# Gate and up biases of 32 experts issued as four products on two row groups, and the scatter's products in alternate order

## The chip, the cores and the metric

The kernel runs on one core of a Trainium2 chip. Its time is the time on the device, in microseconds (us), from the start of the program to its end; lower is better. All times of the trace are of one execution taken by the hardware profiler.

## The reference, cut to what matters

The program is a chain of two transformer blocks on 256 tokens of width 1024: attention and a mixture of experts, then a second block with gated mixers and key-value lookups. Only the mixture of experts is touched. A router picks 4 of 32 experts for each token, with a softmax over the four scores as weights; each expert is a gated feed-forward layer with biases:

```python
def expert_block(args):
    xb, e = args
    gt = xb @ w_gate[e] + b_gate[e]
    up = xb @ w_up[e] + b_up[e]
    gt = jnp.minimum(gt, SWIGLU_LIMIT)
    up = jnp.clip(up, -SWIGLU_LIMIT, SWIGLU_LIMIT)
    hdn = gt * jax.nn.sigmoid(SWIGLU_ALPHA * gt) * (up + 1.0)
    return hdn @ w_down[e] + b_down[e]
...
contrib = ys[dest] * gates.reshape(-1)[order][:, None].astype(ys.dtype)
out = jax.ops.segment_sum(contrib, tok, num_segments=n_tok)
```

All weights are 1024 x 1024 in float32, and all products are float32.

## The kernel before

**Stages.** `program` (line 2998) runs six stages one after the other: `attention`, `route`, `moe`, `peer`, `gla`, `peer`. Each is a block of its own, with one instruction list per engine: TensorE (`pe`), VectorE (`dve`), ScalarE (`act`), GpSimd (`pool`) and SyncE (`sp`), which issues the large DMAs. An engine takes its list in order and waits on semaphores (`wait_ge`). At the end of a block all engines meet.

**Weights.** They stream through a ring of 2 MB slots in SBUF (class `Ring`, line 128): six slots, and five from expert 26 on. SyncE issues the load of a chunk (line 145) as soon as the slot has been given back by the product that read it last. An expert has six chunks: 0 and 1 for gate, 2 and 3 for up, 4 and 5 for down. Eight experts (3, 5, 8, 11, 15, 17, 23, 25) have one more, for work on the context tokens that `Context` (line 745) puts beside the experts.

**An expert on TensorE** (`expert`, in `moe`, from line 1315). 64 slots hold the tokens that chose it. `x.xe` holds their rows, turned. Every product with weights uses 64 columns of the array: the left half of the output's 1024 columns goes to partitions 0 to 63 of a PSUM bank, the right half to partitions 64 to 127 of the same bank, so each weight row gives two products of 512 columns (`halves`, line 1290, products at L1296). In order:

- gate: the biases into bank 4 (L1327), then chunks 0 and 1. The bias product has `x.select` as its stationary operand, [32 rows, 64 columns], of which row e is ones and the others zeros, and the bias table of all 32 experts as its moving operand, [32 rows, 512 columns]; so it writes expert e's bias into all 64 slots. It starts the accumulation in the bank.
- up: the same into bank 5, with chunks 2 and 3. Ahead of its biases stand the wait for `h_ready` of the expert before (VectorE has read bank 5) and `context.wait_left(pe, 5)`, which waits until the work beside the experts has given back bank 5.
- `gather` (L1278) of the next expert's tokens into bank 7, with the one-hot `x.pick`.
- four transposes of `x.h` (L1340) into bank 6.
- `scatter` (L1287) of the expert before: outputs `x.ye`, left halves on rows 0 to 63 and right halves on rows 64 to 127, are added to four accumulators in banks 0 to 3 with `x.weighT` as the stationary operand, [64 rows, 128 columns]. Two products have rows 0 to 63 (token tiles 0 and 1), two have rows 64 to 127.
- two products that turn the weights of this expert's slots (L1347) into bank 4.
- work beside the expert, if there is some (L176, L818, L847, L890), into banks 5 and 7.
- down: chunks 4 and 5 into bank 6.

**On the other engines.** VectorE clamps bank 4 (L1458), makes the one-hots for scatter (L1440), multiplies with the sigmoid (L1463), clamps bank 5 (L1465), makes `x.h` (L1468), copies the next `x.select` out of the identity matrix (`select`, L1435) and makes the next `x.pick` (L1430). ScalarE does the sigmoid (L1391) and copies banks 7, 6, 4 and 6 to SBUF (L1385, L1394, L1398, L1405); the context's results are emptied by ScalarE (L899) or VectorE (L1019, L1033).

**Tables.** `Experts` (line 1051) lays out the arena. `b_gate` and `b_up` are two areas of 1024 columns, each on partitions 0 to 31, loaded in `route` by two DMAs of SyncE's queue. `constants` (line 223) builds a table of constants that is loaded once; its last part, `zero`, is 128 columns wide and is read nowhere.

A second to fourth pass over the experts (`overflow`) runs only when an expert has more than 64 tokens. It does not run in the profiled execution.

The lines of the biases:

```python
for c in range(4):
    bank = 4 + c // 2
    if c % 2 == 0:
        pe.wait_ge(M(name(("weighT_ready", "h_ready")[c // 2], p)), at(p, e, 1))
        if c == 2:
            context.wait_left(pe, 5)
        for n in range(2):
            nc.tensor.matmul(m.ps[n * SLOTS:(n + 1) * SLOTS, bank, :],
                             x.select[0:NE, :],
                             (x.b_gate, x.b_up)[c // 2][0:NE, n * 512:(n + 1) * 512],
                             start=True, stop=False, skip_group_check=True)
```

Of the kernel before, what the change touches and what calls it, by code (L numbers as in the profile page):

```python
# [21 lines left out]
P = 128  # L22
D = 1024
KT = D // P
T = 256
TT = T // P
# [12 lines left out]
NE, TOPK, SLOTS = 32, 4, 64  # L39
# [15 lines left out]
class Marks:  # L55


    def __init__(self, nc, ctx):
        self.nc, self.ctx, self.sems, self.n, self.spare = nc, ctx, {}, {}, []
# [163 lines left out]
def constants():  # L223

    j, i = np.arange(P)[:, None], np.arange(P)[None, :]
    same = (j // CH) == (i // CH)
    parts = {
        "ident": (j == i),
        "upto": (j <= i),
        "ones": np.ones((P, P)),  # L230
        "fwd": (j <= i) & same,
        "bwd": (j >= i) & same,
        "after": (j > i) & same,
        "before": (j < i) & same,
        "chunk": j // CH == np.arange(2)[None, :],
        "iota": np.broadcast_to(np.arange(P) % CH, (P, P)),
        "zero": np.zeros((P, P)),
    }
    return parts

# [810 lines left out]
class Experts:  # L1051


    def __init__(self, m):
        self.yT = m.part(0, KT, T)
        self.router = m.part(4096, KT, NE)
        self.router_b = m.part(4352, NE)
        self.logits = m.part(4384, TT, NE)
        self.gates = m.part(4448, TT, NE)
        self.chosen = m.part(4512, TT, NE)  # L1060
        self.place = m.part(4576, TT, NE + 1)
        self.onehot = m.part(4672, NE)
        self.top = m.part(4704, TT, 8)
        self.top_i = m.part(4720, TT, 8)
        self.top_at = m.arena[:, 4736:4744].bitcast(U32)
        self.exp = m.part(4752, 8)
        self.gatesT = m.part(4800, T)
        self.total = m.part(5056, NE + 2)
        self.b_gate = m.part(5120, D)
        self.b_up = m.part(6144, D)  # L1070
        self.b_down = m.part(7168, D)
        self.pick = m.part(8192, TT, SLOTS)
        self.weigh = m.part(8320, TT, P)
        self.weighT = m.part(8576, T)
        self.xe = m.part(8832, KT, SLOTS)
        self.g = m.part(9344, 512)
        self.sig = m.part(9856, 512)
        self.u = m.part(10368, 512)
        self.h = m.part(10880, 512)
        self.hT = m.part(2048, 4, 2, SLOTS)  # L1080
        self.ye = m.part(2560, 512)
        self.select = m.part(3072, SLOTS)


def route(nc, d, m, M, banks, ring):


    x = Experts(m)
    turn = banks.plan([("t", i) for i in range(4)], [4, 5, 6, 7])
    small = banks.plan([("logit", t) for t in range(TT)] + [("place", t) for t in range(TT)] + ["total", "gT"], [0, 1, 2, 3])  # L1090
    with nc.Block() as block:

        @block.sync
        def _(sp):
            for dst, src in ((x.router, d["router_w"]), (x.router_b[0:1, :], d["router_b"]), (x.b_gate[0:NE, :], d["b_gate"]),
                             (x.b_up[0:NE, :], d["b_up"]), (x.b_down[0:NE, :], d["b_down"])):
                sp.dma_start(dst, src).then_inc(M("router_in"), 16)
            ring.load(sp, ring.at["moe0.0"] + PER_EXPERT)
            sp.dma_start(m.X[:, 2:4, :], d["ctx"].rearrange("(t p) c -> p t c", p=P)).then_inc(M("ctx_in"), 16)
            sp.wait_ge(M("ctx_in"), 16)  # L1100
# [96 lines left out]
def moe(nc, d, m, M, banks, ring):  # L1197
# [3 lines left out]
    x = Experts(m)  # L1201
    context = Context(nc, d, m, M, banks, ring)
# [5 lines left out]
    def name(base, p):  # L1208

        return base if p == 0 else base + "_more"  # L1210

    def at(p, e, base=0):

        return e + base if p == 0 else (p - 1) * NE + e + base
# [7 lines left out]
    def picked(p, e, base=0):  # L1222

        return e + base if p == 0 else (p - 1) * (NE + 1) + e + base
# [7 lines left out]
    with nc.Block() as block:  # L1232
# [32 lines left out]
        def _(pe):  # L1265
            acc = [m.ps[:, 2 * t + n, :] for t in range(TT) for n in range(2)]

            for i in range(4):
                t, n = i // 2, i % 2
                nc.tensor.matmul(acc[i], x.gatesT[0:NE, t * P:(t + 1) * P], x.b_down[0:NE, n * 512:(n + 1) * 512],  # L1270
                                 start=True, stop=False, skip_group_check=True)

            def gather(p, count):

                pe.wait_ge(M(name("pick_ready", p)), count)
                for k in range(KT):
                    for t in range(TT):
                        last = nc.tensor.matmul(m.ps[:, 7, k * SLOTS:(k + 1) * SLOTS], m.X[:, t, k * P:(k + 1) * P],  # L1278
                                                x.pick[:, t, :], start=t == 0, stop=t == TT - 1)
                last.then_inc(M(name("gather_done", p)), 1)  # L1280

            def scatter(ends=False):

                for n in range(2):
                    rows = slice(n * SLOTS, (n + 1) * SLOTS)
                    for t in range(TT):
                        last = nc.tensor.matmul(acc[2 * t + n], x.weighT[rows, t * P:(t + 1) * P], x.ye[rows, :],  # L1287
                                                start=False, stop=ends, skip_group_check=True)
                return last

            def halves(bank, c, w, lhs, first):


                for k in range(KT // 2):
                    for n in range(2):
                        last = nc.tensor.matmul(m.ps[n * SLOTS:(n + 1) * SLOTS, bank, :], lhs(k + KT // 2 * (c % 2), n),  # L1296
                                                w[:, k, n * 512:(n + 1) * 512],
                                                start=first and k == 0, stop=c % 2 == 1 and k == KT // 2 - 1, skip_group_check=True)
                return last
# [3 lines left out]
            def weights(p, c, e):  # L1303
                if p == 0:
                    return ring.wait(pe, f"moe{e}.{c}", k=KT // 2)
                pe.wait_ge(M(f"more_in{c}"), 16 * (at(p, e) + 1))
                return spare[c]

            def used(p, ins, c, e):
                if p == 0:  # L1310
                    ring.used(ins, f"moe{e}.{c}")
                else:
                    ins.then_inc(M(f"more_used{c}"), 1)

            def expert(p, e):
                pe.wait_ge(M(name("select_ready", p)), picked(p, e, 1))

                pe.wait_ge(M(name("xe_ready", p)), picked(p, e, 1))
                for c in range(4):
                    bank = 4 + c // 2  # L1320
                    if c % 2 == 0:

                        pe.wait_ge(M(name(("weighT_ready", "h_ready")[c // 2], p)), at(p, e, 1))
                        if c == 2:
                            context.wait_left(pe, 5)
                        for n in range(2):
                            nc.tensor.matmul(m.ps[n * SLOTS:(n + 1) * SLOTS, bank, :],  # L1327
                                             x.select[0:NE, :],
                                             (x.b_gate, x.b_up)[c // 2][0:NE, n * 512:(n + 1) * 512],
                                             start=True, stop=False, skip_group_check=True)  # L1330
                    w = weights(p, c, e)
                    used(p, halves(bank, c, w, lambda k, n: x.xe[:, k, :], False), c, e)

                context.wait_left(pe, 7)
                gather(p, picked(p, e, 2))

                pe.wait_ge(M(name("h_ready", p)), at(p, e, 2))
                pe.wait_ge(M(name("ye_ready", p)), at(p, e, 1))
                for j in range(4):
                    last = nc.tensor.transpose(m.ps[:, 6, j * P:(j + 1) * P], x.h[:, j * P:(j + 1) * P], m.const("ident"))  # L1340
                last.then_inc(M(name("h_turned", p)), 1)

                scatter().then_inc(M(name("added", p)), 1)

                pe.wait_ge(M(name("weigh_ready", p)), at(p, e, 1))
                for t in range(TT):
                    last = nc.tensor.matmul(m.ps[:, 4, t * P:(t + 1) * P], x.weigh[:, t, :], m.const("ident"), start=True, stop=True)  # L1347
                last.then_inc(M(name("weigh_turned", p)), 1)
                if p == 0:
                    beside.upto(e)  # L1350

                pe.wait_ge(M(name("hT_ready", p)), at(p, e, 1))
                for c in (4, 5):
                    w = weights(p, c, e)
                    used(p, halves(6, c, w, lambda k, n: x.hT[:, k % 4, k // 4, :], c == 4), c, e)
# [65 lines left out]
        def _(dve):  # L1421
# [10 lines left out]

            def select(p, e):

                nc.vector.tensor_copy(x.select[0:NE, :], m.const("ident")[0:NE, bass.ds(e, 1)].to_broadcast([NE, SLOTS]))\  # L1435
                    .then_inc(M(name("select_ready", p)), 1)

            def weigh(p, e):
# [1682 lines left out]
```

## Time and profile before

| | us |
|---|---|
| median of 3 runs | 3803.32 (3801.83 to 3807.24) |
| the profiled execution, its own time | 3807.14 |
| its span, first to last instruction | 3805.3 |
| mean granted TensorE clock over the span | 0.963 of 2.4 GHz |
| TensorE busy | 3356.7 (88% of the span) |
| VectorE busy | 1768.7 (46%) |
| ScalarE busy | 1094.4 (29%) |
| GpSimd busy | 851.4 (22%) |

The durations of instructions come from the one profiled execution, so sums are made against its own 3807.14 us, which lies 3.8 us above the median. Matmuls overlap: the duration of one record reaches beyond the start of the next, and what a product costs is read from the distance between starts. A float32 product appears as two records, each with a load of its stationary operand.

### The profile page before, as it was taken

What the parts mean: (1) busy time and instruction counts of PE and PEld (TensorE: products, weight loads), DVE (VectorE), ACT (ScalarE), POOL (GpSimd) and SP (SyncE); (2) the same over time, 40 slices, a digit from 0 to 9 for tenths busy, and PEclk for the clock granted to TensorE, in tenths of its full rate; (3) what the DMA queues carried; (4) which work ended last, traced back from release to release, by engine and by line L of the source; (5) the groups of instructions that cost most, each with busy time, mean ns of one, the idle gap of its engine ahead of it and who ended that gap; (6) DMA issues with size and microseconds to landing.
All of it is one profiled execution on the core that took longest, in us unless ns stands there. A gap on an engine that the chain in (4) does not pass through costs nothing. (4 is left out here: it accounts for less than half of the span.)

```text
span 3805.3 us, 35526 instructions
## 1 busy us (share of the span) xinstructions
PE 3356.7 (88%) x11828; PEld 1517.6 (40%) x11828; DVE 1768.7 (46%) x4113; ACT 1094.4 (29%) x2964; POOL 851.4 (22%) x796
## 2 busy tenths in 40 slices
PE   8988999999999997898989779898888978877876
PEld 7635444444444443343434323343323544322222
DVE  0053211211121121766776686678753256667664
ACT  0131011111011011443343444444333113434333
POOL 0000000000000000443344344444440004444442
PEclk9999799999999998999999999999999989999999
DMA  6496689999898897999999999999995119999998
GB/s 280 153 384 247 268 368 391 382 380 424 335 428 371 365 411 329 418 422 421 422 418 407 421 402 421 422 421 392 421 421 235 45 36 417 421 421 421 417 414 332
DMA packets 157387, 1380.08 MB, mean 363 GB/s; under 512 B 18505, under 2 KB 19017, under 8 KB 25490
## 3 DMA queue, kind: packets, MB, share of 16 engines
q0 software_dynamic: 111360, 805.46, 51.2%
q1 hardware_dynamic: 45842, 572.29, 36.5%
q8 instruction: 100, 1.64, 0.2%
q14 instruction: 85, 0.70, 0.0%
HBM read 1376.53 MB, written 1.15 MB: 362 GB/s over the span
## 5 line engine op out<-in xcount | busy, mean ns | idle before, releaser
L2595 PE MATMUL ps<-sb_arena,sb_diag 128*128 128x512 f32 x3072 | 1490.1, 624 | 345.7 <-ACT sb_diag L2573 343.7
L2502 POOL DMA_INDIRECT sb_arena<-in_uv,sb_idx x768 | 838.7, 1092 | 2629.3 <-POOLq L1232 1202.5
L2532 DVE SCALAR_TENSOR_TENSOR sb_arena<-sb_arena,sb_H 128x1024 f32<-128x1024 f32 x768 | 940.6, 1226 | 618.4 <-DMA sb_arena<-in_uv,sb_idx 441.9
L2595 PEld LDWEIGHTS ps<-sb_arena,sb_diag 128*128 128x128 f32 x3072 | 563.2, 195 | 1228.8 <-ACT sb_diag L2573 658.8
L1296 PE MATMUL ps<-sb_ring,sb_arena 128*64 128x512 f32 x3072 | 683.1, 597 | 0.0
L2564 ACT ACTIVATE sb_act<-sb_dots 128x1 f32<-128x1 f32 x768 | 155.0, 202 | 1090.8 <-DVE sb_arena L2532 1088.0
L1296 PEld LDWEIGHTS ps<-sb_ring,sb_arena 128*64 128x64 f32 x3072 | 212.6, 137 | 447.0 <-issue 444.8
L2573 ACT ACTIVATE sb_diag<-sb_consts,sb_act 128x128 f32<-128x128 f32 x768 | 308.4, 402 | 26.6 <-PE ps L2595 1.5
L1458 DVE TENSOR_SCALAR sb_arena<-ps 128x512 f32<-128x512 f32 x32 | 22.1, 692 | 609.3 <-PE ps L1296 609.3
L2568 ACT ACTIVATE sb_act<-sb_act,sb_wts 128x1 f32<-128x1 f32 x768 | 226.2, 294 | 24.9
L176 PE MATMUL ps<-sb_ring,sb_arena 128*128 128x512 f32 x480 | 210.8, 598 | 2.7 <-DVE sb_arena L655 1.3
L176 PE MATMUL ps<-sb_H,sb_ring 128*128 128x256 f32 x592 | 132.3, 385 | 13.4 <-DMA sb_ring<-in_w_in 10.7
L176 PEld LDWEIGHTS ps<-sb_ring,sb_arena 128*128 128x128 f32 x480 | 90.8, 192 | 116.6 <-issue 113.7
L1278 PEld LDWEIGHTS ps<-sb_arena,sb_X 128*128 128x128 f32 x1056 | 123.6, 196 | 27.5 <-issue 27.5
L1278 PE MATMUL ps<-sb_arena,sb_X 128*128 128x64 f32 x1056 | 128.2, 281 | 0.0
L176 PEld LDWEIGHTS ps<-sb_H,sb_ring 128*128 128x128 f32 x592 | 113.2, 193 | 32.6 <-issue 17.1
L1385 ACT ACTIVATE sb_arena<-ps 128x512 f32<-128x512 f32 x33 | 19.7, 597 | 353.5 <-PE ps L1278 353.5
L1465 DVE TENSOR_SCALAR sb_arena<-ps 128x512 f32<-128x512 f32 x32 | 22.1, 692 | 187.2 <-PE ps L1296 187.2
L603 DVE SCALAR_TENSOR_TENSOR sb_H<-sb_X,ps 128x128 f32<-128x128 f32 (+1 forms) x56 | 17.8, 348 | 183.7 <-PE ps L405 183.6
L176 PE MATMUL ps<-sb_arena,sb_ring 128*128 128x256 f32 (+1 forms) x480 | 92.0, 352 | 2.2 <-PE ps L176 0.9
L1391 ACT ACTIVATE sb_arena<-sb_arena 128x512 f32<-128x512 f32 x32 | 20.1, 630 | 252.2 <-DVE sb_arena L1458 252.2
L1932 PE MATMUL ps<-sb_ring 128*128 128x512 f32 x192 | 86.3, 592 | 0.0
(337 smaller groups left out, 2313.3 us busy)
## 6 DMA issues: line engine op xcount, KB each, us to landing
sb_ring<-in_moe SPq DMA_DIRECT2D x192, 2048.0 KB, 12.1
sb_ring<-in_w_mod SPq DMA_DIRECT2D x24, 2048.0 KB, 9.1
sb_ring<-in_w_in SPq DMA_DIRECT2D x11, 2048.0 KB, 13.8
sb_ring<-in_a_w_in SPq DMA_DIRECT2D x8, 2048.0 KB, 11.6
sb_ring<-in_b_w_in SPq DMA_DIRECT2D x8, 2048.0 KB, 12.1
sb_ring<-in_w_q SPq DMA_DIRECT2D x6, 2048.0 KB, 9.9
sb_arena<-in_uv,sb_idx POOLq DMA_INDIRECT x768, 15.0
sb_ring<-in_a_w_out SPq DMA_DIRECT2D x4, 2048.0 KB, 11.0
```

The costliest lines, as they stand in the source:

```text
L176: last = nc.tensor.matmul(out, lhs, rhs, start=i == 0, stop=i == len(pairs) - 1)
L1278: last = nc.tensor.matmul(m.ps[:, 7, k * SLOTS:(k + 1) * SLOTS], m.X[:, t, k * P:(k + 1) * P], x.pick[:, t, :], start=t == 0, stop=t == TT ...
L1296: last = nc.tensor.matmul(m.ps[n * SLOTS:(n + 1) * SLOTS, bank, :], lhs(k + KT // 2 * (c % 2), n), w[:, k, n * 512:(n + 1) * 512], start=f ...
L1458: nc.vector.tensor_scalar(x.g, m.ps[:, 4, :], LIMIT, None, ALU.min).then_inc(M(name("g_ready", p)), 1)
L1465: nc.vector.tensor_scalar(x.u, m.ps[:, 5, :], LIMIT, -LIMIT, ALU.min, ALU.max).then_inc(M(name("u_ready", p)), 1)
L1932: last = nc.tensor.matmul(m.ps[:, where[0], :], lhs(k), w[:, k, :], start=k == 0, stop=k == KT - 1)
L2502: pool.indirect_dma_start(uv[n_ % BUFS], None, table, bass.IndirectOffsetOnAxis(m.idx[:, pair % 2, k:k + 1], 0))\
L2532: nc.vector.scalar_tensor_tensor(out=u, in0=u, scalar=1.0, in1=m.H[:, order[i], :], op0=ALU.mult, op1=ALU.mult, accum_out=m.dots[:, n_ % P ...
L2564: nc.scalar.activation(a, m.dots[:, n_ % PK:n_ % PK + 1], ACT.Gelu_apprx_tanh).then_inc(M("gelu_done"), 1)
L2568: nc.scalar.activation(a, a, ACT.Copy, scale=m.wts[:, pair % 2, k:k + 1]).then_inc(M("act_ready"), 1)
L2573: nc.scalar.activation(m.diag[n_ % DIAGS], m.const("ident"), ACT.Copy, scale=a).then_inc(M("diag_ready"), 1)
L2595: last = nc.tensor.matmul(out[h], m.diag[n_ % DIAGS], uv[b][:, D + h * 512:D + (h + 1) * 512], start=opens, stop=ends)
```

## The change

The two bias tables come to lie on top of each other, gate on partitions 0 to 31 and up on partitions 32 to 63 of one area of 1024 columns. `x.select` gets 64 rows instead of 32: row e and row 32 + e are ones. It is copied from a new constant, `expert`, 33 columns wide, that takes the place of the unused `zero`. The four bias products of an expert (left and right half, gate and up) are issued together at its start, alternating between the two groups of 32 rows; all waits for banks 4 and 5 stand ahead of them. In the scatter the two loops are exchanged, so that the products alternate between rows 0 to 63 and 64 to 127.

```diff
-        "zero": np.zeros((P, P)),
+        "expert": (j % NE == i)[:, 0:NE + 1],
...
-        self.b_gate = m.part(5120, D)
-        self.b_up = m.part(6144, D)
+        self.biases = m.part(5120, D)
...
-            for dst, src in ((x.router, d["router_w"]), (x.router_b[0:1, :], d["router_b"]), (x.b_gate[0:NE, :], d["b_gate"]),
-                             (x.b_up[0:NE, :], d["b_up"]), (x.b_down[0:NE, :], d["b_down"])):
+            for dst, src in ((x.router, d["router_w"]), (x.router_b[0:1, :], d["router_b"]), (x.biases[0:NE, :], d["b_gate"]),
+                             (x.biases[NE:2 * NE, :], d["b_up"]), (x.b_down[0:NE, :], d["b_down"])):
...
-                for n in range(2):
-                    rows = slice(n * SLOTS, (n + 1) * SLOTS)
-                    for t in range(TT):
+                for t in range(TT):
+                    for n in range(2):
+                        rows = slice(n * SLOTS, (n + 1) * SLOTS)
                         last = nc.tensor.matmul(acc[2 * t + n], x.weighT[rows, t * P:(t + 1) * P], x.ye[rows, :],
                                                 start=False, stop=ends, skip_group_check=True)
...
+                pe.wait_ge(M(name("weighT_ready", p)), at(p, e, 1))
+                pe.wait_ge(M(name("h_ready", p)), at(p, e, 1))
+                context.wait_left(pe, 5)
+                for n in range(2):
+                    for which in range(2):
+                        rows = slice(which * NE, (which + 1) * NE)
+                        nc.tensor.matmul(m.ps[n * SLOTS:(n + 1) * SLOTS, 4 + which, :], x.select[rows, :],
+                                         x.biases[rows, n * 512:(n + 1) * 512], start=True, stop=False, skip_group_check=True)
                 for c in range(4):
                     bank = 4 + c // 2
-                    if c % 2 == 0:
-
-                        pe.wait_ge(M(name(("weighT_ready", "h_ready")[c // 2], p)), at(p, e, 1))
-                        if c == 2:
-                            context.wait_left(pe, 5)
-                        for n in range(2):
-                            nc.tensor.matmul(m.ps[n * SLOTS:(n + 1) * SLOTS, bank, :],
-                                             x.select[0:NE, :],
-                                             (x.b_gate, x.b_up)[c // 2][0:NE, n * 512:(n + 1) * 512],
-                                             start=True, stop=False, skip_group_check=True)
                     w = weights(p, c, e)
                     used(p, halves(bank, c, w, lambda k, n: x.xe[:, k, :], False), c, e)
...
-                nc.vector.tensor_copy(x.select[0:NE, :], m.const("ident")[0:NE, bass.ds(e, 1)].to_broadcast([NE, SLOTS]))\
+                nc.vector.tensor_copy(x.select[0:2 * NE, :], m.const("expert")[0:2 * NE, bass.ds(e, 1)].to_broadcast([2 * NE, SLOTS]))\
```

## Rows read from the trace of the kernel before

**Rows 1.** The page, its first line: the span.
```profile
span 3805.3 us, 35526 instructions
```

**Rows 2.** Windows: length, busy of PE, PEld, DVE, ACT, POOL, clock, DMA share, GB/s.
```profile
0.00:413.90 413.90, 359.86 (x1782) 234.32 (x1782) 98.04 (x299) 73.04 (x167) 12.69 (x28) 0.91 0.65 255
413.90:1497.00 1083.10, 1082.25 (x5328) 466.26 (x5328) 177.35 (x407) 130.54 (x216) 0.00 (x0) 1.00 0.90 378
1497.00:3805.30 2308.30, 1914.59 (x4720) 816.99 (x4720) 1493.36 (x3407) 890.80 (x2582) 838.70 (x768) 0.96 0.91 375
```

**Rows 3.** Timeline of TensorE, expert 12: start, length, line, records merged into one row.
```profile
835.20 1.07 PE L1327 MATMUL ps<-sb_arena 32*64 32x512 f32 x4
836.21 7.09 PE L1296 MATMUL ps<-sb_ring,sb_arena 128*64 128x512 f32 x32
843.23 1.07 PE L1327 MATMUL ps<-sb_arena 32*64 32x512 f32 x4
844.23 7.09 PE L1296 MATMUL ps<-sb_ring,sb_arena 128*64 128x512 f32 x32
851.25 3.79 PE L1278 MATMUL ps<-sb_arena,sb_X 128*128 128x64 f32 x32
...
855.40 1.99 PE L1287 MATMUL ps<-sb_arena 64*128 64x512 f32 x8
...
857.97 7.09 PE L1296 MATMUL ps<-sb_ring,sb_arena 128*64 128x512 f32 x32
864.99 1.07 PE L1327 MATMUL ps<-sb_arena 32*64 32x512 f32 x4
```

**Rows 4.** Timeline of TensorE in narrow windows: single starts around expert 11's up biases.
```profile
799.17 0.60 PE L1296 MATMUL ps<-sb_ring,sb_arena 128*64 128x512 f32 x2
799.70 0.65 PE L1327 MATMUL ps<-sb_arena 32*64 32x512 f32 x2
...
800.18 0.59 PE L1327 MATMUL ps<-sb_arena 32*64 32x512 f32 x2
800.71 0.65 PE L1296 MATMUL ps<-sb_ring,sb_arena 128*64 128x512 f32 x2
```

**Rows 5.** The same, in expert 11's scatter: its first two records, and its end.
```profile
811.88 0.71 PE L1287 MATMUL ps<-sb_arena 64*128 64x512 f32 x2
...
813.81 0.38 PE L1347 MATMUL ps<-sb_consts,sb_arena 128*128 128x128 f32 x1
```

**Rows 6.** The same: a run of full-array records, the next start, four column groups in attention.
```profile
814.36 13.90 PE L176 MATMUL ps<-sb_ring,sb_arena 128*128 128x512 f32 x32
...
828.19 7.09 PE L1296 MATMUL ps<-sb_ring,sb_arena 128*64 128x512 f32 x32
...
186.83 0.61 PE L420 MATMUL ps<-sb_ring,sb_H 128*2 128x512 f32 x4
```

**Rows 7.** Timeline: what the moved waits wait for; and the line of the picker's copy.
```profile
808.64 0.69 DVE L1468 SCALAR_TENSOR_TENSOR sb_arena<-sb_arena 128x512 f32<-128x512 f32 x1
...
811.35 0.61 PE L1340 MATMUL ps<-sb_consts,sb_arena 128*128 128x128 f32 x4
...
828.35 0.60 ACT L899 ACTIVATE sb_H<-ps 128x512 f32<-128x512 f32 x1 [4.99 <-PE ps L176]
...
L1435 DVE COPY sb_arena<-sb_consts 32x64 f32<-32x64 f32 x31 | 5.4, 175 | 0.0
```

**Rows 8.** Waits of SyncE's queue in the experts; windows of three stretches, columns as in rows 2.
```profile
SPq L145 <- PE ps L1296: 825.8, 185, 16.7
...
1031.00:1037.00 6.00, 6.00 (x17) 2.31 (x17) 0.69 (x1) 0.00 (x0) 0.00 (x0) 1.00 0.00 0
1043.10:1193.80 150.70, 150.70 (x778) 62.79 (x776) 36.28 (x67) 21.39 (x35) 0.00 (x0) 1.00 1.00 424
...
1310.80:1496.20 185.40, 185.35 (x978) 79.47 (x976) 38.39 (x119) 23.65 (x42) 0.00 (x0) 1.00 0.90 375
```

**Rows 9.** Lines by form, 420 to 1470 us: busy us, mean ns of one, idle before.
```profile
L1327 PE MATMUL ps<-sb_arena 32*64 32x512 f32 x248 | 66.6, 613 | 0.0
```

## The prediction

> **What bounds the kernel now.** I read the page first, for the span of the profiled execution [rows 1], then one cut of it into three stretches [rows 2]. The middle one, from 413.9 to 1497.0 us, is the loop over the 32 experts, and the whole diff acts there. The reader should see that TensorE is busy for 1082 of its 1083 us at a granted clock of 1.00, that is 2.4 GHz, and VectorE and ScalarE for 177 and 131 us. So an instruction taken off TensorE's queue there comes off the stretch, unless something new makes TensorE wait. The timeline of one expert without work beside it [rows 3] shows where it goes: two chunks of gate weights (16 products), the up biases, two chunks of up weights, gather, scatter, two chunks of down weights. Last I read single starts around the up biases and in the scatter [rows 4, 5].
>
> How products pack decides everything here. One fp32 product is two records. A full-array record of 512 columns takes its turn for 0.43 us: 32 of them lie between 814.36 and 828.19, 0.432 us each [rows 6]. I call that a slot. Records on different parts of the array share one. The two bias products write the two halves of the columns: their four records start as 799.70 (two of them) and 800.18 (two), so two slots [rows 4]. Four column groups of another stage start four records within 0.02 us of each other (the union of four is 0.61 us, about as long as one) [rows 6]. The scatter's products read rows 0 to 63 and 64 to 127 over all 128 columns: two records start together at 811.88 and the eight are through at 813.81, 1.93 us [rows 5]. One by one they would need eight slots, 3.4 us. So row halves share a slot already, though both products of the first half stand ahead of the second half in the program: the first record of the second half starts beside the first of all.
>
> **The change, part by part.**
> *Gate and up biases together.* Today each pair sits between two runs of 128-row products. The last of them starts at 799.17, the biases at 799.70, the weights again at 800.71, and their next slot follows after 0.48 (as it does inside the bias pair) [rows 4]. Without the up pair these three distances (0.53, 1.01, 0.48) become two slots of 0.43: 2.02 - 0.86 = 1.16 us less, 1.15 with starts that are not rounded. A second reading agrees: 844.23 - 836.21 = 8.02 us for a run of 16 slots with its bias pair, a run of 32 slots with none inside is 7.02 + 16 x 0.43 = 13.9, and 836.21 to 851.25 is 15.04 now [rows 3]: 1.14. Over 32 experts (the 62 pairs of 31 experts are the 248 records of the line [rows 9]; one more expert lies at the edges) this takes off 32 x 1.15 = 36.8 us.
> What comes back: four products in the place of two at the expert's start. Nothing in the trace has two row groups and two column groups at once. Bounds: if all four share slots, only their starts are added, for which the four column groups give 0.02 us at most, and I take 0.013, 0.4 us in all. If nothing shares at all, eight slots stand in the place of two, 6 x 0.43 = 2.6 us each. I take the first: it is nearest to the two rows that show row groups sharing and column groups sharing, every row group keeps its own bank (gate 4, up 5), as in the scatter, and the three second records waiting while the fourth product starts are no more than the scatter has waiting when its second half starts.
> *The scatter's order.* Eight records in four slots is the least that two row halves allow. The alternate order can bring the second start forward by a few ns, below 0.01 us per expert, 0.2 us in all; nor can it lose, since each half again meets the other in another bank. The Trainium skill ("TensorE: Matmul & The Clock Gate", the section on packing small matmuls) says that matmuls run in strict program order and only weight loads are pulled ahead; the trace disagrees, see the rivals.
> *Waits moved to the expert's start.* The up pair's wait for h of the expert before is old by then: that op starts at 808.64, before the transposes at 811.35 that already need it [rows 7]. The wait for bank 5 is the one with less cover. Work beside an expert leaves its last result there, emptied by ScalarE at 828.35 to 828.95 [rows 7], while two chunks of down weights run from 828.19 [rows 6] to 835.20 [rows 3]. Cover 6 us, less if a VectorE op of 0.7 us does it; behind this wait stands the whole TensorE queue, so were the cover gone it would cost all that is late. I take 0.
> *The rest.* VectorE copies 64 rows of the picker instead of 32: 0.17 us now [rows 7], the same columns per row, needed some 25 us later: 0. The bias loads stay two DMAs of the same bytes on SP's queue in the routing stage; the constants shrink by 95 columns of 128 rows. 0.
> *Weights.* The other limit is near. Over five experts without context weights the DMA engines are at share 1.00 and 424 GB/s [rows 8]: 2.10 MB in 4.9 us, 29.7 us for six chunks, against 150.7 / 5 = 30.1 us of TensorE time now and 29.0 after. There the queue falls behind by 0.7 us per expert, 3.5 in all. It enters with a lead: between 1031 and 1037 it moved nothing, all six slots being full [rows 8]. Each slot is worth 4.9 us, so the lead outlasts it. The last six experts have five slots, but 31 us each and a share of 0.90 [rows 8]. SP waited 825.8 us for TensorE to free slots; TensorE for none. I take 0, with 0 to 5 us as bounds.
>
> **Sum.** 36.8 - 0.4 + 0.2 = 36.6 us. The profiled execution took 3807.1 us, 1.8 more than its span [rows 1] and 3.8 more than the median of the runs, 3803.3. So 3770.5 in the profile and 3803.3 - 36.6 = 3766.7 as a median. What a measurement of this kernel can tell from no change is about 0.2%, 7.6 us.
>
> **The rivals.**
> *Three slots.* The second row group gets in one slot late. Saving 1.15 - 0.43 = 0.72, 23.0 us: 3780.3. Against it, the scatter's second half is in its first slot. 6%.
> *Row groups take turns, column pairs stay.* Four slots: 1.15 - 0.86 = 0.29, 9.3 us: 3794.0. It needs 32-row groups to behave unlike 64-row ones. 4%.
> *The other side: the alternate order breaks the column pairs too.* If row groups can't share when columns are split, and a product that can't start holds back the next one, then gate-left, up-left, gate-right, up-right run as 2, 2 and 2 slots (the middle two differ in rows and columns). Six slots, +1.72 against a saving of 1.15: 0.57 us more per expert, 18.2 us: 3821.5. It turns slower as soon as the group passes 2 + 1.15 / 0.43 = 4.7 slots. No row looks like this [rows 5, 6]. 4%.
> *Weights late.* TensorE waits on chunks where the DMA engines are full or the ring has five slots: up to 5 us back, 3772. 9%.
> *A queue in strict order.* Two products of one half ahead of the other half would then need seven slots in the scatter; the alternate order five. Two slots less in 33 scatters is 28 us more gain, 3738. The eight records took four slots' time [rows 5], so there is nothing to collect: 1%. This is what the Trainium skill's rule on program order, named above, would make of it.
> The forecast keeps 76%.
>
> **How the numbers follow.** The main case with a few us of spread between sets of runs gives 3763 to 3771; late weights and the three slots carry the range to 3781, and what is left out is four slots, six slots and strict order, 9%, with the tails. Faster by over 0.2%: main, late weights, three slots, strict order and most of the four-slot case, 0.93; within 0.2%: the rest of that case and an effect unforeseen, 0.03; slower: 0.04.
>
> **What would show it.** One block of eight records of the bias line at each expert's start, lasting as long as today's four (1.07 us), with 1.0 us to the first weight record; 64 records of weights in one run of about 13.9 us behind it; the period of an expert with nothing beside it 28.6 instead of 29.8 us (835.20 to 864.99 [rows 3]); eight records of the scatter still 1.9 us; the middle stretch near 1046.5 us with TensorE idle for under 2 us; the other two stretches as before. Wrong: a bias block of 1.5, 1.9 or 2.8 us (three, four or six slots), or idle time of TensorE ahead of weight products, or ahead of the biases for bank 5.

## The result, and the profile after

| | before | after |
|---|---|---|
| median of all runs, us | 3805.28 (4 runs, 3801.83 to 3809.01) | 3770.23 (4 runs, 3769.16 to 3774.09) |
| ratio | | 0.991, 95% interval 0.9892 to 0.9927 |
| profiled execution, us | 3807.14 | 3770.83 |
| span, us | 3805.3 | 3769.0 |

The change is 35 us faster, 0.9%; the interval reaches from 28 to 41 us. The profiled executions differ by 36.3 us.

The windows of the changed kernel, cut at the same places of the work as [rows 2], the columns too (length, busy time of PE, PEld, DVE, ACT, POOL, clock, DMA share, GB/s):

```profile
0.00:414.30 414.30, 360.53 (x1780) 234.40 (x1781) 98.05 (x299) 73.03 (x167) 12.68 (x28) 0.91 0.65 255
414.30:1459.20 1044.90, 1043.96 (x5328) 462.30 (x5328) 177.46 (x407) 130.57 (x216) 0.00 (x0) 1.00 0.93 392
1459.20:3769.00 2309.80, 1912.74 (x4720) 816.87 (x4720) 1493.18 (x3407) 890.25 (x2582) 846.43 (x768) 0.96 0.91 375
```

The middle stretch lost 38.2 us (1083.1 to 1044.9), the others grew by 0.4 and 1.5. TensorE still runs through without a break. It issues the same number of records, 5328, in less time: nothing was taken away; more of them run at once, and fewer changes of the array's shape lie between them.

The timeline of TensorE for the same expert as [rows 3]:

```profile
820.30 1.09 PE L1324 MATMUL ps<-sb_arena 32*64 32x512 f32 x8
821.32 13.95 PE L1295 MATMUL ps<-sb_ring,sb_arena 128*64 128x512 f32 x64
835.20 3.79 PE L1277 MATMUL ps<-sb_arena,sb_X 128*128 128x64 f32 x32
838.82 0.61 PE L1337 MATMUL ps<-sb_consts,sb_arena 128*128 128x128 f32 x4
839.36 1.99 PE L1286 MATMUL ps<-sb_arena 64*128 64x512 f32 x8
841.28 0.71 PE L1344 MATMUL ps<-sb_consts,sb_arena 128*128 128x128 f32 x4
841.92 7.09 PE L1295 MATMUL ps<-sb_ring,sb_arena 128*64 128x512 f32 x32
848.94 1.09 PE L1324 MATMUL ps<-sb_arena 32*64 32x512 f32 x8
```

Eight bias records, 1.02 us to the first weight record (four took 1.01), then 64 weight records without a break, 13.88 us to the gather. The period is 28.64 us instead of 29.79. The scatter takes 1.92 us (839.36 to 841.28), as before.

Narrow windows of the same timeline show the single starts of the bias block, beside [rows 4]:

```profile
820.30 0.66 PE L1324 MATMUL ps<-sb_arena 32*64 32x512 f32 x4
...
820.78 0.61 PE L1324 MATMUL ps<-sb_arena 32*64 32x512 f32 x4
821.32 0.65 PE L1295 MATMUL ps<-sb_ring,sb_arena 128*64 128x512 f32 x2
```

Four records, one of each product, share the first slot and four the second. In the records of the trace the four starts are 0, 7, 13 and 20 ns after the first. The trace does not say which rows of the array a record uses; that the four are one of each product follows from the run below with both tables on one row group, where four records no longer share a slot.

TensorE's clock in the first expert explains 1.5 us that the change did not make. The windows of 2 us, before and then after:

```profile
416.00:418.00 2.00, 2.00 (x6) 0.55 (x6) 0.00 (x0) 0.00 (x0) 0.00 (x0) 0.50 0.00 0
418.00:420.00 2.00, 2.00 (x6) 0.47 (x4) 0.00 (x0) 0.00 (x0) 0.00 (x0) 0.50 0.00 0
420.00:422.00 2.00, 2.00 (x10) 0.62 (x7) 0.00 (x0) 0.00 (x0) 0.00 (x0) 0.67 0.00 0
```
```profile
416.00:418.00 2.00, 2.00 (x10) 0.56 (x8) 0.00 (x0) 0.00 (x0) 0.00 (x0) 0.50 0.00 0
418.00:420.00 2.00, 2.00 (x10) 0.63 (x8) 0.00 (x0) 0.00 (x0) 0.00 (x0) 0.83 0.00 0
```

The granted clock went from 0.50 to 1.00 (1.2 to 2.4 GHz) inside the third of these windows before, and inside the second after: 7.4 us after the first bias record before, 4.4 us after it in the changed kernel. Three us less at half the clock are 1.5 us of work. So the first expert is shorter by 2.7 us (30.7 us from bias block to bias block, 33.4 before), 1.15 of them the change's. Between the kernels of this study this moved either way: from the first weight record of the first expert to that of the second there are 31.3 us in one kernel with the changed bias block (the alternate quarters below, clock up 7.3 us after the first bias record) and 29.7 in another (the bias block alone, 4.2 us). It is no part of the gain. 38.2 - 1.5 = 36.7 us is.

### The profile page after: what moved, and what is told of

It reads as the page before. It is cut to its first block and busy times, and to the rows that moved or that the text cites. A ratio compares the mean times of both kernels' runs of the same rounds, so it can differ in the third digit from the quotient of the medians.

```text
span 3769.0 us, 35528 instructions
## 1 busy us (share of the span) xinstructions
PE 3317.2 (88%) x11828; PEld 1513.6 (40%) x11828; DVE 1768.7 (47%) x4113; ACT 1093.8 (29%) x2964; POOL 859.1 (23%) x796
## 3 DMA queue, kind: packets, MB, share of 16 engines
q1 hardware_dynamic: 45842, 572.24, 36.7%
HBM read 1376.48 MB, written 1.15 MB: 366 GB/s over the span
## 5 line engine op out<-in xcount | busy, mean ns | idle before, releaser
L1295 PE MATMUL ps<-sb_ring,sb_arena 128*64 128x512 f32 x3072 | 674.5, 595 | 0.0
L1277 PEld LDWEIGHTS ps<-sb_arena,sb_X 128*128 128x128 f32 x1056 | 123.6, 196 | 27.5 <-issue 27.5
L176 PEld LDWEIGHTS ps<-sb_H,sb_ring 128*128 128x128 f32 x592 | 113.5, 193 | 32.6 <-issue 17.1
```

The source lines that it names most:

```text
L176: last = nc.tensor.matmul(out, lhs, rhs, start=i == 0, stop=i == len(pairs) - 1)
```

## The experiments

### Each half of the change alone

The bias block with the scatter as before:

```diff
-                for t in range(TT):
-                    for n in range(2):
-                        rows = slice(n * SLOTS, (n + 1) * SLOTS)
+                for n in range(2):
+                    rows = slice(n * SLOTS, (n + 1) * SLOTS)
+                    for t in range(TT):
```

> The changed kernel with the scatter's two loops back in the order of before. Theory (slots): all of the gain is in the bias block, so the stretch of the experts shortens by 32 x 1.148 = 36.7 us against before and stands within 0.3 us of the changed kernel; the scatter takes 1.92 us either way. Rival (the scatter's order matters, as a queue in strict order would have it): the scatter's eight records stay at 1.92 us but the time is above the changed kernel's by 0.43 us or more per expert, 14 us or more.

Measured: 3767.59 us against 3807.21 for the kernel before, run beside it (the ratios here and in the next section are against those runs), ratio 0.9898 (0.9882 to 0.9915). TensorE's timeline:

```profile
818.61 1.09 PE L1324 MATMUL ps<-sb_arena 32*64 32x512 f32 x8
819.62 13.95 PE L1295 MATMUL ps<-sb_ring,sb_arena 128*64 128x512 f32 x64
...
837.67 1.99 PE L1286 MATMUL ps<-sb_arena 64*128 64x512 f32 x8
839.59 0.71 PE L1344 MATMUL ps<-sb_consts,sb_arena 128*128 128x128 f32 x4
...
847.25 1.09 PE L1324 MATMUL ps<-sb_arena 32*64 32x512 f32 x8
```

The period is 28.64 us too, the scatter 1.92. All of the gain is here.

The scatter's loops exchanged in the kernel before (the same edit the other way):

> The kernel before with the scatter's loops exchanged alone. Theory: 0.006 us per expert, 0.2 us in all, not to be told from nothing in the time, but readable in the starts: the second record starts 0.007 us after the first instead of 0.013. Rival (strict order): 28 us faster. A rival for the other side (the banks of the accumulators collide in the new order): a scatter of over 2 us.

Measured: 3806.42 us, ratio 0.9994 (0.9985 to 1.0004): nothing that the times can tell. In the trace the second record of a scatter starts 7 ns after the first instead of 13, and the scatter takes 1.918 us instead of 1.924, in every expert: 0.2 us in all. Strict order (28 us faster) and colliding banks (slower) both fall.

### Is it the joining, or the sharing by row groups?

The four products together at the expert's start, all waits ahead of them, but both tables left on partitions 0 to 31 (an edit of the kernel before):

```diff
+                for which in range(2):
+                    for n in range(2):
+                        nc.tensor.matmul(m.ps[n * SLOTS:(n + 1) * SLOTS, 4 + which, :],
+                                         x.select[0:NE, :],
+                                         (x.b_gate, x.b_up)[which][0:NE, n * 512:(n + 1) * 512],
+                                         start=True, stop=False, skip_group_check=True)
                 for c in range(4):
...
```

> The four bias products together at the expert's start with all waits ahead of them, as in the change, but both tables on partitions 0 to 31 as before: left and right halves share slots, gate and up can't. Theory: four slots instead of two, a block of 1.88 us to the next weights, period of an expert 0.29 us below before (29.49 against 29.78 us for one with nothing beside it), 9.3 us in all; so of the 1.15 us per expert 0.29 are the shape switch saved and 0.86 the sharing by row groups. Rival (the gain is in joining: fewer switches of the array's shape and fewer waits): 30 to 37 us faster, like the change.

Measured: 3794.83 us, ratio 0.9973 (0.9964 to 0.9983), so 6.5 to 13.7 us faster; the forecast for this run, 9.3, lies inside. TensorE's timeline, a bias block:

```profile
824.26 7.09 PE L1296 MATMUL ps<-sb_ring,sb_arena 128*64 128x512 f32 x32
831.28 1.93 PE L1324 MATMUL ps<-sb_arena 32*64 32x512 f32 x8
833.14 3.23 PE L1296 MATMUL ps<-sb_ring,sb_arena 128*64 128x512 f32 x14
```

The same eight records take 1.86 us to the next weights where the changed kernel has 1.02: four slots instead of two. An expert with nothing beside it takes 29.49 us, 0.29 less than before, 9.4 us over 32. So of the 1.15 us per expert 0.29 come from the joining, that is from the two changes of the array's shape that are saved, and 0.85 from the sharing of slots by the two row groups. In the records, the load of the first stationary operand behind a change of shape starts only 1 to 2 ns ahead of its product; inside a run of weights it starts with the product before, a slot ahead. Whether the late load or something else in the change takes the time was not tested.

The other way round, the row groups without the joining (an edit of the changed kernel: tables, picker of 64 rows and early waits stay, the up biases go back ahead of chunk 2):

```diff
                 for c in range(4):
                     bank = 4 + c // 2
+                    if c % 2 == 0:
+                        which = c // 2
+                        rows = slice(which * NE, (which + 1) * NE)
+                        for n in range(2):
+                            nc.tensor.matmul(m.ps[n * SLOTS:(n + 1) * SLOTS, bank, :], x.select[rows, :],
+                                             x.biases[rows, n * 512:(n + 1) * 512], start=True, stop=False, skip_group_check=True)
```

> The changed kernel, tables on two row groups, picker of 64 rows and all waits at the expert's start, but the up biases issued again ahead of chunk 2. Theory: none of these pieces costs or gains by itself: expert period 29.78 us as before, within 1 us of before in all (the scatter's 0.2 us included). Rival (the early wait for bank 5 costs): idle time of TensorE ahead of the gate biases in the experts after context work, up to 0.7 us each. Rival (rows 32 to 63 are slower or faster for a bias pair by themselves): the pair's 1.00 us changes.

Measured: 3806.56 us, ratio 0.9997 (0.9987 to 1.0006). TensorE's timeline:

```profile
831.55 1.07 PE L1327 MATMUL ps<-sb_arena 32*64 32x512 f32 x4
832.56 7.09 PE L1295 MATMUL ps<-sb_ring,sb_arena 128*64 128x512 f32 x32
839.58 1.07 PE L1327 MATMUL ps<-sb_arena 32*64 32x512 f32 x4
840.58 7.09 PE L1295 MATMUL ps<-sb_ring,sb_arena 128*64 128x512 f32 x32
```

Both pairs take 1.00 to 1.01 us, on rows 0 to 31 and on rows 32 to 63 alike; the period is 29.78 us; TensorE waits for nothing at an expert's start, after context work neither. The early wait for bank 5, the larger picker and the moved table cost nothing. Nor did the wait that stood ahead of the up biases: it is gone from there, and the pair still takes as long, so the 0.29 us of the run before are not a wait saved. Saving needs both: products on two row groups, and beside each other.

### Does the order of the four products matter?

```diff
-                for n in range(2):
-                    for which in range(2):
+                for which in range(2):
+                    for n in range(2):
```

> The changed kernel with the four bias products in the other order: gate left, gate right, up left, up right, so that each row group's column pair stands together. Theory: the order is free within the queue's reach of three waiting records, all four start within 0.02 us, block to the next weights 1.02 us, time as the changed kernel within 1 us. Rival (alternating between row groups matters): up starts a slot late, block 1.45 us, 14 us slower.

Measured: 3767.99 us against 3808.18, ratio 0.9896 (0.988 to 0.9913); the timeline has the same block and run as the changed kernel:

```profile
819.98 1.09 PE L1324 MATMUL ps<-sb_arena 32*64 32x512 f32 x8
821.00 13.95 PE L1295 MATMUL ps<-sb_ring,sb_arena 128*64 128x512 f32 x64
```

The alternation in the bias block is worth nothing either; four starts within 0.02 us in this order as well.

### How far the queue looks past what waits

If the scatter's order is free because TensorE's queue starts a record past three that wait, and past no more, longer runs on one half must lose. Each product of the scatter was cut into two of 256 columns, in the blocked order of before:

```diff
                 for n in range(2):
                     rows = slice(n * SLOTS, (n + 1) * SLOTS)
                     for t in range(TT):
+                        for q in range(2):
+                            cols = slice(q * 256, (q + 1) * 256)
+                            last = nc.tensor.matmul(acc[2 * t + n][:, cols], x.weighT[rows, t * P:(t + 1) * P], x.ye[rows, cols],
+                                                    start=False, stop=ends, skip_group_check=True)
```

> The changed kernel with each of the scatter's products cut into two of 256 columns, in the order of before: four products on rows 0 to 63 (eight records of half a slot), then four on rows 64 to 127. Same arithmetic. Theory (the queue starts a record past three waiting ones, no more, which is what the order of before asks of it): the first record of the second half starts with the fifth of the first half, about 0.95 us late, so 12 half slots in place of 8: the scatter takes 2.8 us instead of 1.92, 0.86 x 33 = 28 us slower than the changed kernel. Rival (the queue looks past any number): 1.9 us, no change. Rival (strict order): the second half starts with the eighth record of the first, 15 half slots, 3.4 us, 48 us slower. Weight loads of 0.19 us per record may hide under the records of 0.21, in all three.

and the same products with `n` as the innermost loop:

> The same 256-column products of the scatter, alternating between the two row halves as the change does. Theory: the alternate order leaves one record waiting, so 8 half slots, 1.9 us, no more than 0.1 us from the changed kernel's scatter, within 3 us of it in time; the difference to the blocked quarters is what the alternate order is worth once the queue is too short, 28 us. Rival (strict order): 9 half slots, 2.1 us. Rival (the cost of quarters is their eight more weight loads): both orders of quarters take the same, longer time.

Measured: blocked 3801.82 us, ratio 0.9983 (0.9973 to 0.9992); alternate 3769.24 us, ratio 0.9902 (0.9886 to 0.9919), both against the same 3808.18 of the kernel before. So the order is worth 32.6 us once there are sixteen records. The scatter in TensorE's timeline, blocked and then alternate:

```profile
851.05 2.96 PE L1288 MATMUL ps<-sb_arena 64*128 64x256 f32 x16
853.95 0.71 PE L1346 MATMUL ps<-sb_consts,sb_arena 128*128 128x128 f32 x4
```
```profile
840.08 2.00 PE L1288 MATMUL ps<-sb_arena 64*128 64x256 f32 x16
842.01 0.71 PE L1346 MATMUL ps<-sb_consts,sb_arena 128*128 128x128 f32 x4
```

2.89 us against 1.93. The single starts of the blocked scatter, in us after its first, read from the records:

```
0  0.320  0.536  0.752  0.967 | 0.973  1.183  1.293  1.399  1.509  1.615  1.725  1.941  2.157  2.372  2.588
```

Five records start alone, one every 0.216 us; 6 ns after the fifth, with the sixth, seventh and eighth of the first half still waiting, the second half begins. The records of one half never share a slot here, which also settles how the scatter of before is to be read: the record that starts 13 ns after its first one belongs to the other half, though the trace does not name the rows. So the reach is the three waiting records that the scatter of before had needed. Each record has its load beside it; whether the limit counts records or records with loads, and whether it is the same for other shapes, no run here separates. I had expected 2.8 us and 28 us in all; it is 2.89 and 32, since the second record of each half starts 0.32 us after the first instead of 0.22, and blocked halves pay that one after the other. The weight loads, twice as many, do not show: the alternate order takes the same 1.93 us with sixteen records as the changed kernel with eight. Strict order would have given 3.4 us here.

### How near the weights are

The four bias products left out (gate and up biases are then missing from the result), the first weight product of a bank starting it:

```diff
-                for n in range(2):
-                    for which in range(2):
-                        rows = slice(which * NE, (which + 1) * NE)
-                        nc.tensor.matmul(m.ps[n * SLOTS:(n + 1) * SLOTS, 4 + which, :], x.select[rows, :],
-                                         x.biases[rows, n * 512:(n + 1) * 512], start=True, stop=False, skip_group_check=True)
...
-                    used(p, halves(bank, c, w, lambda k, n: x.xe[:, k, :], False), c, e)
+                    used(p, halves(bank, c, w, lambda k, n: x.xe[:, k, :], c % 2 == 0), c, e)
```

> The changed kernel without the four bias products of the experts (the gate and up biases are left out of the result; the first product of a bank starts it). It asks how much more TensorE time can go before the weights come too late. Theory: per expert another block with its switches, about 1.16 us, goes, 37 us if all weights were there in time; the slack of the weights (3.6 us at the tightest in the changed kernel) is then used up in the long runs of experts without context work and in the last six, so 5 to 20 us of idle time of TensorE ahead of weight products: 17 to 32 us faster than the changed kernel, 3738 to 3753. Rival (weights were never near): no idle time, 37 us faster. Rival (weights already bind in the changed kernel): under 5 us faster.

Measured: 3734.62 us, ratio 0.9809 (0.9792 to 0.9825); 35.6 us below the changed kernel's median, which comes from other runs, and 33.4 below the kernel with the bias products in the other order, which ran beside it. I missed this one: next to no idle time came. The waits of TensorE in the experts:

```profile
PE ps L1295 <- DMA sb_ring<-in_moe: 0.8, 2, 0.4
```

Two waits, 0.8 us. But the margin is gone exactly there. In the records, the tightest chunk landed 6.1 us ahead of its first product before, 3.6 us ahead in the changed kernel, and two chunks (the up weights of experts 23 and 31) just in time here. The timeline at the first of them:

```profile
1149.59 3.65 PE L1295 MATMUL ps<-sb_ring,sb_arena 128*64 128x512 f32 x16 [0.30 <-DMA sb_ring<-in_moe]
```

The same stretch of five experts without context weights as in [rows 8], in the changed kernel and then here:

```profile
1021.30:1166.30 145.00, 145.00 (x782) 62.27 (x780) 36.30 (x67) 21.40 (x35) 0.00 (x0) 1.00 1.01 428
```
```profile
999.70:1138.80 139.10, 139.10 (x738) 61.69 (x736) 36.31 (x67) 21.39 (x35) 0.00 (x0) 1.00 1.01 428
```

The rate is at its end, 428 GB/s in both; chunks land every 4.9 us, 29.4 us for an expert that TensorE finishes in 27.5 to 28.3. The stretch lives on the lead that the ring built up beside the context work ahead of it, and uses all of it. My 5 to 20 us had taken the tightest slack of the changed kernel as the lead of the whole stretch; it is larger at the stretch's start (17 us for the first chunk of expert 18 here).

## Why the prediction was right, point by point

The measured 3770.2 us lie in the range, 3763 to 3781, and the mechanism is the forecast's main case.

**The bound.** TensorE was the bound, as [rows 2] had it, and stayed it: what left its timeline left the time.

**The saving of 1.15 us per expert.** Confirmed to some ns: all experts but the first have periods shorter by 1.15 us (expert 12 with 29.79 and 28.64), with context work beside them or without. Both parts of the term, switches and slots, have their own run: 0.29 and 0.85.

**The two row groups by two column groups**, the one thing that no row had shown, share slots as the rows of one kind each had suggested; the two added starts cost 0.013 us per block, as taken. Three, four and six slots all fall with the block of 1.02 us. The four-slot case is what a kernel gets that joins the products without moving a table, and there it measured 1.86 us.

**The scatter.** Worth 0.2 us by its starts, as forecast; the times can't tell it from nothing. The reading behind it, that the second half was in its first slot already because the queue reaches past three waiting records, was put to the test and held; the Trainium skill ("TensorE: Matmul & The Clock Gate", the section on packing small matmuls) has matmuls in strict program order, and the trace disagrees: in the kernel before, the second half starts 13 ns after the first record, ahead of three waiting ones of the first half.

**The moved waits, picker and table.** Nothing, shown by the run with the groups apart. The picker's copy took 179 ns where it was 175:

```profile
L1432 DVE COPY sb_arena<-sb_consts 64x64 f32<-64x64 f32 x32 | 5.7, 179 | 0.0
```

**The weights.** They stayed in time, at 3.6 us of slack. The size of the margin had been argued from rates alone, and the forecast worried about the wrong place: it did its sum for the five experts without context weights and took the last six for safe at 31 us each, but the least slack is that of expert 31's up weights (6.9 us before, 3.6 after), and of the ten tightest chunks of the changed kernel nine are in those last six experts, where the ring has five slots. The rate that I took for the engines' limit, 424 GB/s, was not quite it: 428 came.

**The sum.** 3766.7 us forecast, 3770.2 measured. The forecast was made against a median of three runs, 3803.3; with the fourth it is 3805.3, which is 2 us of the 3.5. In the profile 3770.5 was forecast and 3770.8 came. That it is so close is partly luck: 1.5 us came from the clock in the first expert and 1.9 us were lost outside the experts, where the diff touches only the loads of the tables and constants; neither was in the forecast, and they cancel.

## What to carry to other kernels

Products with few rows that stand alone between full-array products cost twice: their slots, and the change of shape around them. Put them beside each other, on different row groups and into different banks (one bank for both was not tried), and they cost one pair of slots, provided that the banks are free that early. Before reordering small products for overlap, look at their single starts: a pair that starts together already has nothing left to give, and an alternate order pays only where runs on one row group grow long (four records here cost nothing, eight did; five to seven were not run). And when the busiest engine gets faster, measure the slack of the transfers behind it: here a second gain of the same size still went through but for 0.8 us, with the last of the margin.

## What the runs showed of the hardware

- Four products on two groups of 32 rows by two groups of 64 columns start within 0.020 us and run at once: eight records of 512 columns in 1.02 us, against 1.86 us where they lie on one row group.
- A record can start past three earlier ones that wait for another row group, and not past a fourth: with eight records of 0.216 us ahead, the other half began with the fifth. Measured for two groups of 64 rows over 128 columns.
- A change of the array's shape costs 0.09 us going in (0.52 instead of 0.43 us between starts) and 0.05 us after the first record (0.48 instead of 0.43), for these shapes (32 rows between runs of 128, 64 columns each); joining two blocks saved both twice, 0.29 us.
- Half-length records (256 columns) with a weight load of 0.19 us each cost nothing extra where two row groups alternate: 1.93 us against 1.92.
- 428 GB/s is what the 16 DMA engines gave at a share of 1.01, when the ring kept them busy throughout: one chunk of 2 MB every 4.9 us.
